# High and low half of x as one 512-column operand of the gate and up projections

## The reference, cut to what matters

```python
def swiglu_ffn(x, w_gate, w_up, w_down):
    return (jax.nn.silu(x @ w_gate) * (x @ w_up)) @ w_down

def hybrid_layer(x, ...):
    x = x + 0.5 * swiglu_ffn(rms_norm(x, ffn1_norm), ffn1_w_gate, ffn1_w_up, ffn1_w_down)
    proj = rms_norm(x, mix_norm) @ w_in
    ...                                   # Hyena, latent attention and gated linear attention
    x = x + jnp.concatenate([y_hy, y_mla, y_gla], axis=-1) @ w_out
    x = x + 0.5 * swiglu_ffn(rms_norm(x, ffn2_norm), ffn2_w_gate, ffn2_w_up, ffn2_w_down)
    return x
```

## Time and profile before

| | before |
|---|---|
| median of 3 runs | 1089.12 us (1088.06 to 1089.48) |
| span of the profiled execution | 1087.3 us |
| TensorE busy, matmuls | 1053.6 us (97%), 7148 |
| VectorE busy | 587.2 us (54%) |
| ScalarE busy | 493.3 us (45%) |
| weight slots fetched | 163 of 1 MB |

### The profile page before, as it was taken

The page is one execution under the profiler, slowest core; times in us unless marked ns, Lnnn a source line. Parts: engine busy times, 40 slices in busy tenths (PEclk is TensorE's granted clock), DMA queues, the critical chain, the costliest instruction groups (busy, mean ns, idle before and its releaser), DMA issues.

```text
span 1087.3 us, 18211 instructions
## 1 busy us (share of the span) xinstructions
PE 1053.6 (97%) x7148; PEld 949.8 (87%) x7148; DVE 587.2 (54%) x630; ACT 493.3 (45%) x656; POOL 103.5 (10%) x165
## 2 busy tenths in 40 slices
PE   6999999999989999999989999999998999999996
PEld 6999999778768999999889999998796789999995
DVE  4644454755665654445465544457456655445544
ACT  6443344447434544443364344335555354433342
POOL 2000000330341000000010000005004210000000
PEclk9999999999979999999999999999999899999999
DMA  9565455253212455545545555554252126554551
GB/s 327 197 219 186 182 190 193 80 192 140 106 56 88 158 191 193 193 169 182 191 166 197 191 193 187 181 173 148 99 181 78 39 79 232 187 183 174 190 204 48
DMA packets 26277, 178.38 MB, mean 164 GB/s; under 512 B 3152, under 2 KB 3664, under 8 KB 5360
## 3 DMA queue, kind: packets, MB, share of 16 engines
q1 hardware_dynamic: 24912, 174.73, 44.3%
q0 software_dynamic: 880, 2.74, 0.8%
q10 hardware_dynamic: 432, 0.18, 0.1%
HBM read 176.94 MB, written 1.05 MB: 164 GB/s over the span
## 4 chain that ended last, share of the span: by engine, by line
PE 63%; issue 28%; POOL 5%; ACT 1%; DVE 1%; DMA 1%; POOLq 0%; DVEq 0%; SPq 0%; ACTq 0%
PE psum L882 20%; PE psum L883 20%; PE psum L884 20%; POOL mixer_scratch L306 3%; PE psum L1103 1%; PE psum L899 1%; DMA w_raw<-in_w_dram 1%; PE psum L972 1%; ACT w_high L367 1%; POOL statistics L283 1%; POOL mixer_scratch L333 0%; POOL mixer_scratch L338 0%; POOL statistics L293 0%; ACT mixer_scratch L438 0%; PE psum L967 0%
## 5 line engine op out<-in xcount | busy, mean ns | idle before, releaser
L588 DVE TENSOR_TENSOR w_low<-w_raw,w_high 128x2048 fp32r<-128x2048 f32 x163 | 375.3, 2305 | 245.7 <-ACT w_high L367 245.7
L882 PE MATMUL psum<-xT_high,w_high 128*128 128x256 f32 x1536 | 436.1, 284 | 5.4 <-DVE xT_low L593 4.5
L883 PE MATMUL psum<-xT_low,w_high 128*128 128x256 f32 x1536 | 434.6, 283 | 0.0
L884 PE MATMUL psum<-xT_high,w_low 128*128 128x256 f32 x1536 | 434.6, 283 | 0.0
L367 ACT ACTIVATE w_high<-w_raw 128x2048 fp32r<-128x2048 f32 x163 | 311.1, 1914 | 124.9 <-PE psum L884 119.9
L882 PEld LDWEIGHTS psum<-xT_high,w_high 128*128 128x128 f32 x1536 | 294.6, 192 | 8.9 <-DVE xT_low L593 5.3
L883 PEld LDWEIGHTS psum<-xT_low,w_high 128*128 128x128 f32 x1536 | 294.6, 192 | 1.5
L884 PEld LDWEIGHTS psum<-xT_high,w_low 128*128 128x128 f32 x1536 | 294.6, 192 | 0.0
L396 ACT ACTIVATE silu_gate<-psum 128x256 f32<-128x256 f32 x88 | 33.7, 383 | 273.1 <-PE psum L884 273.1
L882 PE MATMUL psum<-w_high,hT_high 128*128 128x512 f32 (+1 forms) x360 | 139.9, 389 | 0.0
L883 PE MATMUL psum<-w_low,hT_high 128*128 128x512 f32 (+1 forms) x360 | 139.7, 388 | 0.0
(11 more groups left out here) (163 smaller groups left out, 804.9 us busy)
## 6 DMA issues: line engine op xcount, KB each, us to landing
w_raw<-in_w_dram SPq DMA_DIRECT2D x163, 1024.0 KB, 4.8
x<-in_x_dram SPq DMA_DIRECT2D x2, 512.0 KB, 4.3
mixer_scratch<-in_fil_dram POOLq DMA_DIRECT2D x2, 512.0 KB, 6.8
out_dram<-x_normed SPq DMA_DIRECT2D x4, 256.0 KB, 2.1
mixer_scratch<-in_fil_dram POOLq DMA_DIRECT2D x2, 384.0 KB, 7.4
mixer_scratch<-in_fil_dram POOLq DMA_DIRECT2D x2, 352.0 KB, 5.9
dft<-in_dft_dram SPq DMA_DIRECT2D x1, 512.0 KB, 6.8
inverse_dft<-in_dft_dram SPq DMA_DIRECT2D x1, 512.0 KB, 6.5
```

The costliest lines, as they stand in the source:

```text
L588: e.tensor_tensor(WL[p][:], raw[p][:], WH[p][:].bitcast(F32), ALU.subtract).then_inc(s_lo.sem, 1)
L882: e.matmul(out, ah, bh, start=start, stop=False)
L883: e.matmul(out, ah, bl, start=False, stop=False)
L884: return e.matmul(out, al, bh, start=False, stop=stop)
```

## The change

High and low x now lie side by side in one tile, `xT_split`, of 2 x 256 columns per k tile. In gate/up the high weights are loaded once per k tile and multiply both, a matmul of 512 columns (`split_passes`); the low weights multiply high x as before. Of three matmuls and weight loads per k tile two are left, with the same sum of columns. The result of a group fills a whole bank: columns 0 to 255 hold (high w x high x) + (low w x high x), columns 256 to 511 hold high w x low x. Gate and up thus take two banks, 4 and 5 for half 0 and 6 and 7 for half 1, the same ones in each chunk.

The two halves must be added. Only one operand comes from PSUM: ACT copies the second halves of both banks to `part` (new `part_copy`), DVE adds the first halves to `both` (new `add_parts`), and silu and gate read `both`. TensorE waits for `parts_added` before it writes a half's banks again. The filter's two matmuls use banks 3 and 4 in place of 7.

```diff
@@ -104,8 +104,8 @@
         WL = [sb(f"w_low{i}", [P, 4, 512], F32R) for i in range(RING)]
         x = sb("x", [P, T, D])
         xn = sb("x_normed", [P, T, D])
-        XH = sb("xT_high", [P, KD, SEQ], F32R)
-        XL = sb("xT_low", [P, KD, SEQ], F32R)
+        XB = sb("xT_split", [P, KD, 2, SEQ], F32R)
+        XH, XL = XB[:, :, 0, :], XB[:, :, 1, :]
         sg = sb("silu_gate", [P, 2, SEQ])
         hid = sb("hidden", [P, 2, SEQ])
         HHB = [sb(f"hT_high{i}", [P, 2, SEQ], F32R) for i in range(2)]
@@ -161,6 +161,7 @@
         NV = view(3, T, 256)
         KT = view(2, T, DR)
         assert cols[0] <= 16896, cols[0]
+        part, both = NV[:, 0], NV[:, 1]
 
         fil = scratch[:, 0:NFIL]
         at = NFIL
@@ -184,6 +185,7 @@
...
+        s_part, s_both = mark("part_copied", 4 * CH), mark("parts_added", 4 * CH)
...
@@ -391,9 +393,13 @@
                     turned_high(l, turn, g, g, (2 * g, 2 * g + 1), col)
                 hi(l, slot + 1)
 
-            def silu(l, q, f, pr, slot):
+            def part_copy(l, q, f, slot):
                 e.wait_ge(s_used.sem, used(l, slot))
-                e.activation(sg[:, f, :], PS[:, 4 + 2 * pr + f, 0:SEQ], ACT.Silu).then_inc(s_silu.sem, 1)
+                e.activation(part, PS[:, 4 + 2 * f:6 + 2 * f, SEQ:2 * SEQ], ACT.Copy).then_inc(s_part.sem, 1)
+
+            def silu(l, q, f):
+                e.wait_ge(s_both.sem, s_both.at(l, 2 * q + f + 1))
+                e.activation(sg[:, f, :], both[:, 0, :], ACT.Silu).then_inc(s_silu.sem, 1)
 
             def ht_high(l, q, f, pr):
                 e.wait_ge(s_h.sem, s_h.at(l, 2 * q + f + 1))
@@ -412,9 +418,10 @@
 
                     q = f * CH + (c - 1)
                     for h in range(2):
-                        silu(l, q, h, 1 - pr, base + h if c is first else base + 3 * c - 4 + h)
+                        part_copy(l, q, h, base + h if c is first else base + 3 * c - 4 + h)
                         if c is not first:
                             hi(l, base + 3 * c - 1 + h, (pos(base + 2 + h), base // RING + c - 1 + (2 + h) // RING + 1))
+                        silu(l, q, h)
                         ht_high(l, q, h, 1 - pr)
                     hi(l, base + 3 * c + 1, (pos(base + 1), base // RING + c + 1))
                 first = 1
@@ -426,10 +433,12 @@
                     chunk(i * 2 + 3, 1)
                 chunk(CH - 1, (CH - 1) % 2)
                 q, pr = f * CH + CH - 1, (CH - 1) % 2
-                silu(l, q, 0, pr, base + FFN_SLOTS - 4)
+                part_copy(l, q, 0, base + FFN_SLOTS - 4)
                 hi(l, base + FFN_SLOTS - 1)
+                silu(l, q, 0)
                 ht_high(l, q, 0, pr)
-                silu(l, q, 1, pr, base + FFN_SLOTS - 3)
+                part_copy(l, q, 1, base + FFN_SLOTS - 3)
+                silu(l, q, 1)
                 ht_high(l, q, 1, pr)
                 if f == 0:
                     sine(l, 1, H2)
@@ -605,7 +614,11 @@
 
             def gate(l, q, f, pr):
                 e.wait_ge(s_silu.sem, s_silu.at(l, 2 * q + f + 1))
-                e.tensor_tensor(hid[:, f, :], sg[:, f, :], PS[:, 4 + 2 * pr + f, SEQ:2 * SEQ], ALU.mult).then_inc(s_h.sem, 1)
+                e.tensor_tensor(hid[:, f, :], sg[:, f, :], both[:, 1, :], ALU.mult).then_inc(s_h.sem, 1)
+
+            def add_parts(l, q, f):
+                e.wait_ge(s_part.sem, s_part.at(l, 2 * q + f + 1))
+                e.tensor_tensor(both, PS[:, 4 + 2 * f:6 + 2 * f, 0:SEQ], part, ALU.add).then_inc(s_both.sem, 1)
 
             def ht_low(l, q, f, pr):
                 e.wait_ge(s_hh.sem, s_hh.at(l, 2 * q + f + 1))
@@ -645,27 +658,30 @@
                 def chunk(c, pr):
                     q = f * CH + (c - 1)
                     for h in range(2):
-                        gate(l, q, h, 1 - pr)
+                        add_parts(l, q, h)
                         if c is not first:
                             lo(l, base + 3 * c - 1 + h, pos(base + 2 + h))
+                        gate(l, q, h, 1 - pr)
                         ht_low(l, q, h, 1 - pr)
                     lo(l, base + 3 * c + 1, pos(base + 1))
                 first = 1
                 if f == 0:
-                    argument(l, 0, 7, C_FB1, C_FF1)
+                    argument(l, 0, 3, C_FB1, C_FF1)
                 chunk(first, 1)
                 with e.Fori(0, (CH - 3) // 2) as i:
                     chunk(i * 2 + 2, 0)
                     chunk(i * 2 + 3, 1)
                 chunk(CH - 1, (CH - 1) % 2)
                 q, pr = f * CH + CH - 1, (CH - 1) % 2
+                add_parts(l, q, 0)
+                lo(l, base + FFN_SLOTS - 1)
                 gate(l, q, 0, pr)
-                lo(l, base + FFN_SLOTS - 1)
                 ht_low(l, q, 0, pr)
+                add_parts(l, q, 1)
                 gate(l, q, 1, pr)
                 ht_low(l, q, 1, pr)
                 if f == 0:
-                    argument(l, 1, 7, C_FB2, C_FF2)
+                    argument(l, 1, 4, C_FB2, C_FF2)
                     lo(l, S_G3)
                 else:
                     lo(l, SLOTS)
@@ -883,6 +899,11 @@
                 e.matmul(out, ah, bl, start=False, stop=False)
                 return e.matmul(out, al, bh, start=False, stop=stop)
 
+            def split_passes(out, half, ah, al, k):
+
+                e.matmul(out, ah, XB[:, k, :, :], start=k == 0, stop=False)
+                return e.matmul(out[:, 0:SEQ], al, XH[:, k, :], start=False, stop=k == KD - 1)
+
             def turn_group(l, j, g, bank, tiles):
                 for n, k in enumerate(tiles):
                     for t in range(T):
@@ -953,8 +974,7 @@
                         if first:
                             x_tile(l, turn, k, g == 0)
                         a = slice((k % 2) * 256 + g * P, (k % 2) * 256 + (g + 1) * P)
-                        r = passes(PS[:, 4 + 2 * pr + half, g * SEQ:(g + 1) * SEQ], WH[p][:, k // 2, a], WL[p][:, k // 2, a],
-                                   XH[:, k, :], XL[:, k, :], k == 0, k == KD - 1)
+                        r = split_passes(PS[:, 4 + 2 * half + g, :], half, WH[p][:, k // 2, a], WL[p][:, k // 2, a], k)
                 r.then_inc(s_used.sem, 1)
 
             def filter_mm(l, n, w, src, rows_, bank):
@@ -979,17 +999,20 @@
 
                 def chunk(c, pr, first=False):
                     q = f * CH + (c - 1)
+                    e.wait_ge(s_both.sem, s_both.at(l, 2 * q + 1))
                     gate_up(l, turn, base + 3 * c - 1, pos(base + 2), 0, pr, False)
+                    e.wait_ge(s_both.sem, s_both.at(l, 2 * q + 2))
+                    gate_up(l, turn, base + 3 * c, pos(base), 1, pr, False)
+
+                    if f == 0 and c is last:
+                        e.wait_ge(s_both.sem, s_both.at(l, 2 * q + 3))
+                        filter_mm(l, 1, F_W2, H1, HYF, 4)
                     if f == 0 and first:
                         e.wait_ge(f_arg.sem, f_arg.at(l, 1))
-                    gate_up(l, turn, base + 3 * c, pos(base), 1, pr, False)
-
-                    if f == 0 and c is last:
-                        filter_mm(l, 1, F_W2, H1, HYF, 7)
                     down(l, base + 3 * c + 1, pos(base + 1), q, 1 - pr, first, False, f)
                 last = CH - 1
                 if f == 0:
-                    filter_mm(l, 0, F_W1, fil[:, F_Z:F_Z + SEQ], HYE, 7)
+                    filter_mm(l, 0, F_W1, fil[:, F_Z:F_Z + SEQ], HYE, 3)
                 chunk(1, 1, True)
                 with e.Fori(0, (CH - 3) // 2) as i:
                     chunk(i * 2 + 2, 0)
```

## The result

The changed kernel takes 1090.38 us (median of 9 runs, 1089.77 to 1092.75) against 1089.12 us: ratio 1.0021, 95% interval 1.0012 to 1.0031. By the ratio it is 1.3 to 3.4 us slower. I had forecast 1079.2 us, 10 us faster.

What follows compares the result with a forecast made beforehand. The kernel was taken as bound by how fast TensorE can start matmuls. Span 1087.3 - 17.5 (merging) + 7.2 (stalls) + 0.4 (end of FFN1) = 1077.4 us, plus 1.8 gives 1079.2 us; range 1073 to 1088.

Steps and rivals of the forecast that it cites:

- I take 347.: Gate/up: a pair (one matmul of 512, one of 256) takes 347 ns, not 359.7; 1376 pairs save 17.5 us.
- three prices for a pair (341, 347, 355): Gate/up, ns per pair by cost of the width seams: savings of 25.7, 17.5 or 6.5 us.
- The high end of my bounds (355): Gate/up: every seam paid in full, 355 ns a pair, gain 6.5 us, kernel at 1090.2 us; chance 0.12.
- The stall, +7.2 us.: Start of each FFN1: DVE's add queues behind the sine's argument, so TensorE stalls 3.6 us, once per layer.
- The clock.: Rival: TensorE's clock falls to half after the FFN1 stalls, long or short; no clock loss in the sum.
- a long drop: After each FFN1 stall, half clock as long as in the mixer: 6.8 us lost twice, 1092.9 us; chance 0.06.
- a short one: After each FFN1 stall, half clock for 3 to 4 us, 2 us lost each, 1081 to 1083 us; chance 0.14.
- The end of FFN1, +0.4 us.: End of FFN1: last copy and add delay the second argument 1.3 us, 1.1 absorbed, 0.2 us left per layer.
- The steady state and FFN2's start, 0.: Loop and FFN2 start: copy and add hidden beside TensorE, with 5 us and 0.6 us of cover; cost 0.

Runs made afterwards that it cites:

- e4: The changed kernel with its copy, add, waits and banks, but unmerged: three matmuls of 256 columns per k tile; 1100.04 us, ratio 1.0089 to the kernel before.
- e6: The changed kernel with the first add ahead of the filter's argument and two matmuls of 512 columns, then two of 256, in turn; 1073.08 us, ratio 0.9862.
- e2: The changed kernel with chunk 0's half 0 add moved ahead of the filter's argument at the start of FFN1; 1081.10 us, ratio 0.9925 to the kernel before.
- e7: The changed kernel with chunk 0's half 0 add in the middle of the filter's argument, behind its third of seven operations; 1086.29 us, ratio 0.9977.
- e3 again: Unchanged repeat of the changed kernel with early first add and eight matmuls of 512 columns, then eight of 256; 1077.07 us, ratio 0.9897.
- e3: The changed kernel with the first add ahead of the filter's argument and eight matmuls of 512 columns, then eight of 256; 1076.76 us, ratio 0.9889.
- e6 again: Unchanged repeat of the changed kernel with early first add and 512s and 256s in turn by twos; 1072.81 us, ratio 0.9845 to the kernel before.
- e5: The changed kernel with the first add ahead of the filter's argument and all 16 matmuls of 512 columns of a slot before its 16 of 256; 1076.17 us.
- e8: The changed kernel with early first add, turns of two in each part's first two slots, elsewhere 16 of 512 then 16 of 256; 1071.67 us, ratio 0.9834.
- e1: The changed kernel with eight matmuls of 512 columns, then eight of 256, in a column group instead of alternating pairs; 1088.14 us, ratio 0.9984.

## Why the prediction was wrong

- **"I take 347."** This step failed, the term of the merging. I had three prices for a pair (341, 347, 355) and let the dearer start at one seam be offset by the cheaper one at the other. Under strict alternation it isn't: a 512 is followed after 236 ns (in place of 227), and the 256 after 117, which gives back only 3 of these 9. That is 353.3 ns, in all steady slots. The saving is 359.7 - 353.3 = 6.4 ns, times 1376 = 8.8 us in place of 17.5. e4 measures 7 to 10 us for the same term. The down slot behind the alternation, slower by 0.03 to 0.04 us (some 1.3 us over the 36 steady chunks), was not in the sum at all: a chunk gains 0.19 us where 0.41 was forecast. The high end of my bounds (355) was nearer, and the rows for it, 0.23 and 0.24 us behind each other in the earlier trace rows, were read and then argued away. What the rows support is that the first 512s after a change run slow (0.23 and 0.24 us). That alternation keeps TensorE in that state fits them, but e6 at 348 ns shows that this alone is not the rule.
- **The stall, +7.2 us.** Right: 3.62 us in each layer, by the cause named, and gone with e2.
- **The clock.** I gave 0.06 to a long drop and 0.14 to a short one and left its price out of the sum. It fell in both layers, for 3.5 us, 1.5 us of loss each: 3.0 us. The rival was right in kind and near the short drop's 2 us in size; the chance was too low. I had set the hole against one of 1.91 us that did no harm. One such hole proves little: e7 shows that 2.2 us can be enough, and e2's profiled run has a drop behind 1.90 us.
- **The end of FFN1, +0.4 us.** Small as said. The norm's first matmul of the mixer has 0.18 us of idle time ahead of it, ended by DVE's diagonal, where there was none. It starts 0.77 us after the matmul ahead of it in place of 0.71, which makes 0.1 us in both layers.
- **The steady state and FFN2's start, 0.** Right for the waits: no wait for the parts but the two, 0.6 us of cover in FFN2 as forecast, and e4 has the old pace of 120 ns with all additions in place.
- **The sum redone.** 1087.3 - 8.8 + 7.2 + 3.0 + 0.1 = 1088.8 us of span, against 1088.3 in the profile. The first mixer stage gained 1.0 us that I had not in the sum. Its stretch at half clock, which answers to the earlier trace rows, begins later:

```profile
305.00:310.00 5.00, 3.19 (x28) 1.96 (x28) 3.26 (x5) 1.31 (x5) 3.93 (x10) 0.83 0.00 0
310.00:315.00 5.00, 5.00 (x23) 2.82 (x24) 2.68 (x3) 1.76 (x6) 3.38 (x6) 0.50 0.02 3
```

Nothing in the mixer was changed, so this moves from run to run by a us or two, and it limits what single us can be told apart here.

The two misses, 8.7 and 3.0 us, both turn the same way and are together the 12 us that turned a gain of 10 into a loss of 1 to 3. The range (to 1088) ended below the measured time because I treated them as rivals one at a time: at its measured size each alone gives at most 1088 (1079.2 + 8.7 and 1079.2 + 3.0), both together don't.

**What stays open.** Why strict alternation is slower than turns of two. In the profiled run of the change the first two slots of both FFN1 parts ran at 347 ns a pair (from 20.11 to 26.35 us 18 pairs in 6.24 us), with the same instructions that take 353 in the later slots and in FFN2. So TensorE has at least two paces for one and the same sequence, and which one it falls into was not settled. The profiled runs with strict alternation (the change, e2, e7) show only where each stood: every gate/up slot behind a down slot went at 353, and 347 was seen ahead of a part's first down slot alone, in some parts and not in others. Also open is what makes a hole of some 2 us cost the clock in one run and not in the next.

## What to carry to other kernels

When a change alters the sequence of matmuls, price it from a stretch with that very sequence; two steady paces and the seams between them don't give the pace of an alternation. Group equal widths, by twos at least, and look at what the grouping does where TensorE waits tile by tile.

When banks lose their double buffer, go through the first round apart from the steady state: the operation that frees a bank must stand in its engine's queue ahead of everything that isn't urgent. Price a new hole with the half-clock stretch that can come behind it, and add up the misses that can happen together before drawing the range.

## What the runs showed of the hardware

- One sequence of matmuls, two paces: pairs of 512 and 256 columns at 347 or at 353 ns, each held over a whole slot and more, at the same granted clock of 1.00.
- The clock can fall late: after the hole of 3.62 us in layer 1 TensorE ran at 2.4 GHz for another 0.8 us before it went to 1.2 GHz, in layer 2 for 1.3 us, and so the loss falls on matmuls that look unrelated to the hole. Not always: in e4's profiled run the clock fell at 30.7 us, inside the same hole (it ended at 31.75), and stayed at half until 37.5. The Trainium skill ("TensorE: Matmul & The Clock Gate", section "HAM oscillation — how this bites in real kernels") describes such drops between bursts; the trace agrees, with 3.5 us at half clock and 1.5 us lost.
- The length of a hole did not decide by itself. At the start of layer 2's FFN1 holes of 1.82, 1.88, 1.90, 2.02 and 2.05 us stood ahead of a drop (e3 again, e3, e2, e6 again, e5), and holes of 1.80, 1.82, 1.82, 1.82, 2.04 and 2.12 us (e6, e8, the change, e4, e1, e7) did not.
- The mixer's half-clock stretch isn't fixed either. In layer 1 it is there in the runs before and after (the earlier trace rows and the rows above), and in the profiled run of e8, whose time of 1067.87 us is the lowest of all, it is missing:

```profile
305.00:310.00 5.00, 3.70 (x40) 2.89 (x42) 3.54 (x5) 2.27 (x9) 2.56 (x6) 1.00 0.00 0
```

- The widths' price: 120 ns for 256 columns (e4) and 227 for 512, but 347 to 353 for one of each, by the order and, in strict alternation, by the pace that TensorE is in.
